# RWKV-7 block inverses on 32x32 tiles, HGRN outer products on two row tiles, and a final norm folded into narrow tiles

## What is computed

```python
for i in range(DEPTH):                      # 4
    h = rms_norm(x, W['norm_mix'][i])
    # i % 3: 0 hgrn2_mixer, 1 diff_attn_mixer, 2 rwkv7_mixer
    x = x + mixed
    x = x + swiglu(rms_norm(x, W['norm_ffn'][i]), W['ffn_w_in'][i], W['ffn_w_out'][i])
y = rms_norm(x, W['final_norm'])

# RWKV-7, per token:
sk = einsum('bhij,bhj->bhi', S, kkt)
S = S * wt[:, :, None, :] - sk[..., None] * (kkt * at)[:, :, None, :] + vt[..., None] * kt[:, :, None, :]
# HGRN2, per chunk:
S = exp(b_last)[..., None] * S + einsum('bhsk,bhsv->bhkv', kc * exp(b_last - b), vc)
```

## Time and profile before

| | |
|---|---|
| runs shown | 3472.07, 3476.20, 3477.99 us; median 3476.2 |
| the profiled execution | 3473.62 us, its span 3472.0 us |
| TensorE busy | 3318.1 us, 96% of the span |
| VectorE, ScalarE, GpSimd busy | 54%, 30%, 4% |
| mean granted clock of TensorE | 0.976 |

### The profile page before, as it was taken

How to read it: one execution, slowest core, us unless ns; L and a number is a source line. 1 busy time by engine, 2 the same in 40 slices (tenths; PEclk the granted TensorE clock), 3 DMA queues, 4 the chain that set the end, 5 groups by cost and what they waited for, 6 DMA issues and landing times.

```text
span 3472.0 us, 77052 instructions
## 1 busy us (share of the span) xinstructions
PE 3318.1 (96%) x32788; PEld 3153.8 (91%) x32788; DVE 1884.0 (54%) x2949; ACT 1055.3 (30%) x1674; POOL 131.4 (4%) x247
## 2 busy tenths in 40 slices
PE   8999999999998999997999999999999999899997
PEld 7998899998787999996988777899999999799997
DVE  5666643445655543437457776543345666654343
ACT  3222322223555321222434343332223222232221
POOL 0000000001322000000000000000000000000000
PEclk9999999999999999999999999899999999899999
DMA  3222222222433222221200000222222222122221
GB/s 124 85 82 74 68 85 91 85 95 94 129 120 97 86 94 82 85 92 58 83 21 16 19 11 14 61 89 93 83 91 86 74 80 74 62 86 92 84 92 67
DMA packets 103584, 269.40 MB, mean 78 GB/s; under 512 B 12690, under 2 KB 45714, under 8 KB 103010
## 3 DMA queue, kind: packets, MB, share of 16 engines
q1 hardware_dynamic: 90338, 228.94, 20.3%
q0 software_dynamic: 13056, 37.64, 3.2%
HBM read 248.01 MB, written 18.52 MB: 77 GB/s over the span
## 4 chain that ended last, share of the span: by engine, by line
PE 81%; DVE 10%; ACT 3%; DVEq 3%; issue 2%; SPq 0%; DMA 0%; ACTq 0%
PE ps L559 64%; PE ps L985 5%; PE ps L660 3%; PE ps L977 1%; PE ps L1081 1%; PE ps L691 1%; PE ps L707 1%; DVE cell L2166 1%; DVE arena_r L1873 1%; DVE arena L2033 1%; PE ps L685 1%; DVE rstd L1852 1%; DVEq L2165 1%; DVE h L2163 0%; DVE arena_r L1879 0%
## 5 line engine op out<-in xcount | busy, mean ns | idle before, releaser
L559 PE MATMUL ps<-arena_r 128*128 128x272 f32 x11136 | 1499.7, 293 | 66.4 <-DVE arena_r L1866 21.3
L559 PEld LDWEIGHTS ps<-arena_r 128*128 128x128 f32 x11136 | 1433.3, 191 | 108.3 <-issue 60.2
L559 PE MATMUL ps<-hb_r,arena_r 128*128 128x272 f32 x8448 | 1060.6, 288 | 0.4 <-DVE hb_r L1866 0.4
L559 PEld LDWEIGHTS ps<-hb_r,arena_r 128*128 128x128 f32 x8448 | 1058.4, 188 | 1.2 <-DVE hb_r L1866 0.9
L1368 ACT ACTIVATE arena_r<-ring 128x1024 fp32r<-128x1024 f32 (+1 forms) x240 | 275.4, 1148 | 913.3 <-PE ps L559 913.3
L1892 DVE TENSOR_TENSOR arena_r<-ring,arena_r 128x1024 fp32r<-128x1024 f32 (+1 forms) x240 | 319.7, 1332 | 142.9 <-ACT arena_r L1368 142.9
L1932 DVE TENSOR_TENSOR arena<-ps,rstd 128x544 f32<-128x544 f32 x88 | 63.8, 725 | 292.8 <-PE ps L559 292.8
L1953 DVE TENSOR_TENSOR x<-x,ps 128x544 f32<-128x544 f32 x64 | 46.2, 722 | 293.8 <-PE ps L559 293.8
L1350 ACT ACTIVATE arena_r<-ring 128x1024 fp32r<-128x1024 f32 x80 | 84.6, 1058 | 227.3 <-PE ps L559 221.9
L660 PE MATMUL ps<-arena 128*128 128x128 f32 x1024 | 141.0, 282 | 9.2 <-DVE arena L1996 6.8
L660 PEld LDWEIGHTS ps<-arena 128*128 128x128 f32 x1024 | 129.7, 196 | 13.1 <-issue 7.3
(11 more groups left out here) (386 smaller groups left out, 3077.7 us busy)
## 6 DMA issues: line engine op xcount, KB each, us to landing
ring<-in_w_up SPq DMA_DIRECT2D x176, 512.0 KB, 3.5
ring<-in_w_mix SPq DMA_DIRECT2D x112, 512.0 KB, 3.5
ring<-in_w_down SPq DMA_DIRECT2D x64, 704.0 KB, 4.0
arena<-in_hg_s POOLq DMA_DIRECT2D x16, 512.0 KB, 3.7
out_hg_so<-arena POOLq DMA_DIRECT2D x16, 512.0 KB, 2.9
ring<-in_w_hgout SPq DMA_DIRECT2D x16, 512.0 KB, 3.4
arena<-in_cache_k SPq DMA_DIRECT2D x128, 64.0 KB, 1.8
arena<-in_cache_v POOLq DMA_DIRECT2D x128, 64.0 KB, 2.2
```

The lines of the kernel that those rows point to most:

```text
L559: mm = pe.matmul(PS[:, 2 * a + hf, 0:HALF], part[:, ws], rhs[:, o:o + HALF], start=start and n == 0, stop=stop and n == 2)
```

## The change

Three independent edits.

1. **RWKV inverses.** The 32x32 diagonal blocks of the 64x64 matrices are gathered into compact arrays: 128 partitions are four quarters of 32 (two heads, upper and lower block), and 8 chunks of 32 columns. X and XT lie side by side in one 512-column array. Levels 1 to 4 run on these, on four diagonal 32x32 tiles, and one VectorE operation updates both. Level 5 joins the two blocks of a head: two products of 32x32 blocks between quarters, whose result is written with a minus sign into the upper right part of XT, while ScalarE puts the compact blocks onto its diagonal (`diagonal`). `update(5)` moves ahead of the tensor `rw_at` on VectorE. The constants shrink from 768 columns of level masks to 320 + 34.
2. **HGRN outer products.** The last 32 columns of the values and keys are copied once more behind themselves, so that their transposes fill 64 rows; `hg_vx` has 64 rows and 4 x 128 columns, and the two matmuls use rows 0 to 31 and 32 to 63.
3. **Final norm.** The last chunk's squares are added by the matmul itself. The sum over partitions is made in four column tiles, each with its quarter of the tokens, so root and reciprocal work on 136 columns; four matmuls spread the quarters to all partitions, and VectorE multiplies straight from PSUM. The output leaves in eight transfers.

```diff
+C1 = C2 // 2
...
+        rw_xc, rw_xtc = ([b[:, n * MC:(n + 1) * MC] for b in rw_x] for n in range(2))
+        rw_mtc = [b[:, 0:MC] for b in rw_xt]
...
+        rw_quarters = [slice(q * C1, (q + 1) * C1) for q in range(4)]
+        rw_halves = tuple(zip(rw_quarters[0::2], rw_quarters[1::2]))
...
-            sp.wait_ge(S("norm_h"), KC * (nth_plain("nfin") + 1))
-            sp.dma_start(T["y"], H[:, :]).then_inc(S("y_out"), 16)
+            for c in range(KC):
+                cs = slice(c * NT, (c + 1) * NT)
+                sp.wait_ge(S("norm_h"), KC * nth_plain("nfin") + c + 1)
+                sp.dma_start(T["y"][:, cs], H[:, cs]).then_inc(S("y_out"), 16)
...
-                    pe.transpose(PS[0:NS_TOK, 7, 0:P], hg_v[:, NP_TOK:NT], const("ident")).then_inc(S(L + "vt_mm"), 1)
+                    pe.transpose(PS[0:2 * NS_TOK, 7, 0:P], hg_v[:, NP_TOK:NT + NS_TOK], const("ident")).then_inc(S(L + "vt_mm"), 1)
...
                     for g in range(2):
-                        mm = pe.matmul(PS[:, 6 + g, :], hg_kts[0:NS_TOK, :], hg_vx[0:NS_TOK, g * 512:(g + 1) * 512],
-                                       start=True, stop=True)
+                        rows = slice(g * NS_TOK, (g + 1) * NS_TOK)
+                        mm = pe.matmul(PS[:, 6 + g, :], hg_kts[rows, :], hg_vx[rows, :], start=True, stop=True)
...
+                def by_block(bank, at, a, b):
+                    for n in range(N2):
+                        cs = slice(n * C1, (n + 1) * C1)
+                        for q in rw_quarters:
+                            mm = pe.matmul(PS[q, bank, at + n * C1:at + (n + 1) * C1], a[q, cs], b[q, cs], start=True, stop=True)
+                    return mm
...
-                        by_chunk(4, rw_ml[s], rw_x[s]).then_inc(S("rw_y_mm"), 1)
+                        if lv < 5:
+                            by_block(4, 0, rw_ml[s], rw_xc[s]).then_inc(S("rw_y_mm"), 1)
+                            return
+                        for n in range(N2):
+                            cs = slice(n * C1, (n + 1) * C1)
+                            for top, low in rw_halves:
+                                mm = pe.matmul(PS[low, 4, cs], rw_mt[s][top, n * C2 + C1:(n + 1) * C2], rw_xc[s][top, cs],
+                                               start=True, stop=True)
+                        mm.then_inc(S("rw_y_mm"), 1)
...
                         if lv < 5:
-                            by_chunk(6, rw_xt[s], rw_y[s])
-                        by_chunk(7, rw_y[s], rw_xt[s]).then_inc(S("rw_xy_mm"), 1)
+                            by_block(6, 0, rw_xtc[s], rw_y[s])
+                            by_block(6, MC, rw_y[s], rw_xtc[s]).then_inc(S("rw_xy_mm"), 1)
+                            return
...
+                            for top, low in rw_halves:
+                                mm = pe.matmul(PS[top, 7, cs], rw_y[s][low, cs], rw_xtc[s][low, cs], start=True, stop=True)
...
+                src = nm_sq[(KC - 1) % 2] if last else nm_acc
+                for q in range(4):
+                    mm = pe.matmul(PS[q * 32:(q + 1) * 32, 0, 0:NT // 4], const("ones")[:, 0:32], src[:, q * (NT // 4):(q + 1) * (NT // 4)],
+                                   start=not last, stop=bool(last), skip_group_check=True)
...
+                mm = pe.matmul(PS[:, 4 + q, 0:NT // 4], const("ones")[rows, :], rstd[rows, 0:NT // 4], start=True, stop=True)
...
-                    act.activation(rw_y[h % 2], PS[:, 4, :], ACT.Copy).then_inc(S("rw_y_ev"), 1)
+                    act.activation(rw_y[h % 2][:, 0:MC], PS[:, 4, 0:MC], ACT.Copy).then_inc(S("rw_y_ev"), 1)
+
+                def diagonal(h):
+                    s = h % 2
+                    xt, xtc = (ap.rearrange("p (n c) -> p n c", n=N2) for ap in (rw_xt[s], rw_xtc[s]))
+                    act.activation(xt[:, :, 0:C1], xtc, ACT.Copy, scale=const("half")[:, 0:1])
+                    for top, low in rw_halves:
+                        act.activation(xt[low, :, C1:C2], xtc[low, :, :], ACT.Copy)
...
                     level(h, 5)
+                    diagonal(h)
...
+                    if k == 2:
+                        last = dve.tensor_tensor(hg_v[:, NT:NT + NS_TOK], PS[:, 1, HALF - NS_TOK:HALF], rstd[:, NP_TOK:NT], ALU.mult)
...
+                            if n == 3:
+                                dve.tensor_copy(hg_ks[:, NT:NT + NS_TOK], hg_ks[:, NP_TOK:NT])
...
                     dve.wait_ge(S("rw_mat_mm"), upto(MAT, "m", n))
-                    dve.tensor_tensor(mat(rw_x[s]), mat(PS[:, 1, :]), every(lvl(0, 0)), ALU.mult).then_inc(S("rw_masked"), 1)
+                    dve.scalar_tensor_tensor(xc, m[:, :, 0:C1], top, every_block(lvl(0, 0)), ALU.mult, ALU.mult)
+                    dve.scalar_tensor_tensor(xtc, m[:, :, C1:C2], low, every_block(lvl(0, 0)), ALU.mult, ALU.mult)\
+                       .then_inc(S("rw_masked"), 1)
...
-                    return dve.tensor_tensor(mat(rw_ml[h % 2]), mat(rw_mt[h % 2]), every(lvl(lv, 1)), ALU.mult)
+                    return dve.tensor_tensor(blocks(rw_ml[h % 2][:, 0:MC]), blocks(rw_mtc[h % 2]), every_block(lvl(lv, 1)), ALU.mult)
...
                         if lv < 5:
-                            dve.tensor_tensor(rw_x[s], rw_x[s], PS[:, 6, :], ALU.subtract)
-                        dve.tensor_tensor(rw_xt[s], rw_xt[s], PS[:, 7, :], ALU.subtract).then_inc(S("rw_inv"), 1)
+                            dve.tensor_tensor(rw_x[s], rw_x[s], PS[:, 6, :], ALU.subtract).then_inc(S("rw_inv"), 1)
+                            return
+                        for top, low in rw_halves:
+                            last = dve.tensor_scalar(mat(rw_xt[s])[top, :, C1:C2], blocks(PS[top, 7, 0:MC]), -1.0, None, ALU.mult)
+                        last.then_inc(S("rw_inv"), 1)
...
-                    next_mask(4)
...
+                    update(5)
+
                     dve.tensor_tensor(mat(rw_at[s]), eye, pc.to_broadcast([P, N2, C2]), ALU.mult)
-                    update(5)
...
-            norm("nfin", x3, V_FIN)
+            dve.reciprocal(rstd[:, 0:NT // 4], rstd[:, 0:NT // 4]).then_inc(S("fin_r"), 1)
+            dve.wait_ge(S("fin_mm"), 1)
+            for c in range(KC):
+                dve.scalar_tensor_tensor(h3[:, c, :].rearrange("p (q t) -> p q t", q=4), x3[:, c, :].rearrange("p (q t) -> p q t", q=4),
+                                         vec3[:, V_FIN, c:c + 1], PS[:, 4:8, 0:NT // 4], ALU.mult, ALU.mult).then_inc(S("norm_h"), 1)
```

More of the change, by code:

```diff
@@ L122, in constants @@
     put("dist", np.where(j <= q, -(q - j).astype(np.float64), NEG))
[L123 to L128, removed]
+    lv = np.zeros((P, 5, 2, C1))
+    s1, u1 = s % C1, u[:, 0:C1]
+    for n in range(5):
+        off = (s1 >> (n + 1) == u1 >> (n + 1)) & (s1 >> n != u1 >> n)
+        lv[:, n, 0] = off & (s1 > u1)
+        lv[:, n, 1] = off & (s1 < u1)
+    put("lvl32", lv.reshape(P, -1))
+    put("eye32", s1 == u1)
+    put("half", np.concatenate([s < C1, s >= C1], 1))
     put("low", s > u)
@@ L272, in build @@
         ar.take(shared)
-        hg_sgp, hg_sgn, hg_qs, hg_qr, hg_v, hg_gs = (ar.take(NT) for _ in range(6))
-        hg_f, hg_q, hg_qp, hg_ks = (ar.take(NT) for _ in range(4))
+        hg_sgp, hg_sgn, hg_qs, hg_qr = (ar.take(NT) for _ in range(4))
+        hg_v, hg_gs = ar.take(NT + NS_TOK), ar.take(NT)
+        hg_f, hg_q, hg_qp, hg_ks = (ar.take(w) for w in (NT, NT, NT, NT + NS_TOK))
         hg_d = ar.take(NT)
@@ L278, in build @@
         hg_kt, hg_kts = ar.take(NP_TOK), ar.take(P)
-        hg_vx = ar.take(NB * P)
+        hg_vx = ar.take(NB // 2 * P)
         hg_s = ar.take(NCH * P)
@@ L1320, in _ @@
                 feed_forward(layer)
-            norm("nfin", 0)
+            for last in range(2):
+                if last:
+                    pe.wait_ge(S("norm_sq"), KC * nth("nfin") + KC)
+                else:
+                    pe.wait_ge(S("norm_acc"), sums("nfin") + KC - 2)
+                src = nm_sq[(KC - 1) % 2] if last else nm_acc
+                for q in range(4):
+                    mm = pe.matmul(PS[q * 32:(q + 1) * 32, 0, 0:NT // 4], const("ones")[:, 0:32], src[:, q * (NT // 4):(q + 1) * (NT // 4)],
+                                   start=not last, stop=bool(last), skip_group_check=True)
+            mm.then_inc(S("norm_ssq"), 1)
+            pe.wait_ge(S("fin_r"), 1)
+            for q in range(4):
+                rows = slice(q * 32, (q + 1) * 32)
+                mm = pe.matmul(PS[:, 4 + q, 0:NT // 4], const("ones")[rows, :], rstd[rows, 0:NT // 4], start=True, stop=True)
+            mm.then_inc(S("fin_mm"), 1)
         @block.scalar
@@ L1838, in _ @@
                 feed_forward(layer)
-            root("nfin", 0)
+            act.wait_ge(S("norm_ssq"), nth("nfin") + 1)
+            act.activation(rstd[:, 0:NT // 4], PS[:, 0, 0:NT // 4], ACT.Sqrt, scale=1024.0 / D, bias=scratch[:, 1:2])\
+               .then_inc(S("norm_rms"), 1)
         @block.vector
         def _(dve):
-            def norm(name, src, gain):
-                factor(name)
```

(3 more changed lines are left out.)

72 lines of the change are left out of this document (49 added, 23 removed).

## The result

The kernel after takes **3487.1 us** (median of six, 3485.4 to 3489.4) against 3475.8 us before (six, 3472.1 to 3478.0): ratio 1.0034, 95% interval 1.0021 to 1.0047. It is 0.3% slower, which is clear of the spread, and outside my range (3405 to 3465 us); the profiled execution has a span of 3485.9 us against 3472.0.

A forecast was written before the change was run, and what follows sets the result against it. TensorE, busy 96% of the span, was taken as the bound. RWKV 30, HGRN 13 and the end 7.5 us gave 50.5 off 3473.6, so 3423, stated as 3425 us; range 3405 to 3465.

The forecast's parts named there:

- starting them is no bound: RWKV four-tile 32x32 products: records start every 8 ns, so 64 records take 0.54 us in place of 0.92.
- if instructions don't come fast enough (twice as many in a product): Closing condition for the forecast being wrong, on the new 32x32 products; no size or chance given.
- records at 29 ns: Rival: starting a record is the limit, a product takes 1.84 us, total 3540 us; chance 0.03.
- 2 to 3: RWKV pair, level 2 to level 3: from 5.92 us to 5.2.
- 1 to 2: RWKV pair, level 1 to level 2: from 7.03 us, product start to product start, to 5.7.
- The product and the changes of shape: RWKV levels: a 32x32 product takes 0.54 us, each change of tile shape loses 0.15, in all 0.9 a pair.
- ScalarE's chain: RWKV levels 3 and 5: ScalarE's work comes next as limit, so even a product at no cost gains little more.
- The clock: RWKV pairs: a second clock drop in every second pair, costing 2 us, allowed as 1.0 us a pair.
- level 4 to 5: RWKV pair, level 4 to level 5: from 6.01 us to 4.5.
- The clock's rival: RWKV levels: the clock stays low through the levels, a pair gets 11 us longer, total 3504 us; chance 0.09.
- The overlap: HGRN's two outer products overlap on two row tiles, 0.95 us for 1.90; 13 us over 16 heads, range 0 to 15.
- The end: Final norm and output: smaller root and reciprocal, eight transfers, ending 7.5 us earlier, range 6 to 8.5.

The follow-up runs named there:

- level 5 alone: Kernel before with only level 5 as 32x32 products, its copy and update half as large, mask gone, update moved ahead: 3466.1 us, ratio 0.9979.
- half the products: Kernel after with the compact products of levels 1 to 4 over only four of eight chunks: 3419.1 us, 0.9846 of before.
- the probe: Kernel before plus unused 32x32 and 64x64 products behind TensorE's last work, straight and looped: 32x32 records 27 to 31 ns straight, 12 ns looped.
- The extra product: Kernel before with the HGRN and final norm edits, one outer product done once more per head: 3468.6 us, ratio 0.9982.
- RWKV alone: Kernel before with only the RWKV part of the change: 3509.1 us, ratio 1.0095, runs from 3499.9 to 3511.7.

## Why the prediction was wrong

**The step that failed** is "starting them is no bound". I took 8 ns a record from a row of 0.10 us with some twelve records and used it for stretches of 260. The closing sentence had the case ("if instructions don't come fast enough (twice as many in a product)"), and I gave it neither a price nor a chance. The rival nearest to it, records at 29 ns, had the right rate for the wrong reason: it put the limit into starting each record, where it would hold always, and so gave 3540. The limit is an average over a packet, 256 instructions in 3.47 us at best, behind a few hundred read ahead. It can be priced from my own order of issue. Levels 1 to 5 hold 228, 260, 248 and 208 records in their four stretches, 1,888 instructions, 7.4 packets: 25.6 us. I had 20.45, and 27.25 were measured. The floor falls where it should: 2 to 3 has the most instructions for its time and took 9.2 for 5.2, while 1 to 2 comes behind products that draw instructions more slowly and took 5.64 for 5.7. Had I written the fetches beside the times, the forecast would have been 5 us a pair higher, a gain of the whole near 10 us and not 50. From there to the measured loss of 11, HGRN's missing 12 us and what the levels took above that floor (1.6 us a pair, 13 in all, the clock's part with it) are enough.

**The product and the changes of shape.** Right: 0.54 and 0.15 us against 0.67 together, and 0.15 again at level 5 alone. One reading on the way was not: L1063 loads 32 columns and also moves only 32, so the step from 57 to 36 ns can't tell that the load's width sets the pace. Two other rows of before can. With 64 columns loaded and 4 moved (L1127) a tile takes 58 ns, with 32 loaded and 64 moved (L1086) 56: the wider of the two sets it. Both are 32 in the new product, so the price did not suffer.

**ScalarE's chain.** Right as the next limit, 1.1 us of wait ahead of the sample inverse in the pair from 1930 after, 1.68 with half the products.

**The clock.** The term was too small. The RWKV stage has 0.86 for 0.92 before (the same 465 us), which is 56 us more at 1.2 GHz, 7 a pair, where I had allowed 3.4 us in every second pair. The dips now fall on the levels: with half the products, level 4 to 5 still takes 6.26 us for some 3.7 by my terms, its rate product of 1.1 us taking 1.5. The stops for instructions are not their only cause, since with the stops gone the clock is 0.86 as well; the wait for ScalarE that I had named stands ahead of the dip in the pair shown. Of the 50 us by which RWKV missed, 37 are stops of the product queue; the rest I put down to the clock by elimination; no run separates the two. The clock's rival, that small products themselves are too little work to bring it back, fell: in the loop of the probe they did.

**HGRN.** The overlap was right (0.85 for 0.95). The sum was not: 1 us came of 13. A dip of 1.5 us in five of the twelve heads, where there was none before, took back most of it. The extra product leaves two dips of five, and kernels with heads of 41 us have at most two, which fits an exchange of saved time for dips; why a dip comes in one head and not in the next is not shown.

**The end.** Right in each term.

**Left open:** 2.1 us between the HGRN layer and RWKV, and the 14 us by which the parts miss their sum. Dips moved in time and the spread of RWKV alone are what I would suspect; no run pins it.

## What to carry to other kernels

Count instructions, not only time, where straight code packs small products: two per record, 256 in about 3.5 us, and no more than some 390 ran ahead here. A stretch that wants them faster is bound by its fetches, and here half the tile meant twice the instructions. Take small tiles where they keep the count (level 5, the outer products, the last norm), and be wary where they double it in a dense stretch. And a saving on a full TensorE is only as good as the clock behind it: read the heads or pairs one by one, since a mean hides a saving of 0.8 and a dip of 1.5.

## What the hardware showed that I had not expected

- A packet of 256 instructions arrives every 3.47 us at best, 27 ns a record; 390 instructions ran before the first stop. A loop of 256 instructions drew one packet at its start and none after, and HGRN's loop of some 630 records a head none in 270 us.
- 32x32 products of f32 on four tiles run at 10 ns a record in the kernel with the change of shape behind them, far below the 29 of 64x64 ones on two.
- With TensorE stopped for instructions half of the time, the granted clock was 0.50 for 62 us.
- Sixteen 4-column records in 1.8 us were followed by no dip in twelve heads of 41.0 us before, and by one of 1.5 us in five of twelve heads of 40.3 after.
